# Prompt attention rewritten as one pipeline over heads and groups

## The chip, the cores and the metric

One core of a Trainium2 chip runs one program. The metric is the device time of one execution in microseconds (us), lower is better. TensorE (PE) multiplies matrices from the on-chip memory SBUF into the accumulators PSUM (eight banks), VectorE (DVE), ScalarE (ACT) and GpSimd (POOL) work on elements, and SyncE (SP) issues DMA transfers. All wait for each other by semaphores only.

## The reference, cut to what matters

The program is one inference step of a decoder layer for a prompt of 512 tokens and 32 sampled tokens. All arithmetic is float32. The part that matters here is attention over the prompt:

```
proj = rmsnorm(x) @ w_in           # queries, keys, values, gates of two mixers
# (B) differential attention, 8 heads, two maps each
a = softmax(q1 k1' * s + bias) - lam * softmax(q2 k2' * s + bias)   # causal, 512 x 512
o_b = rmsnorm(a @ v, subln_g) * (1 - lam_init)
# (A) sparse attention, 16 heads in 4 groups that share keys; three branches each
o_c = softmax(q kc' * s + bias) @ vc     # 32 compressed rows
o_s = softmax(q ks' * s + bias) @ vs     # selected blocks: at 512 tokens all of them, causal
o_w = softmax(q kw' * s + bias) @ vw     # the last 512 tokens, causal
o_a = g0 * o_c + g1 * o_s + g2 * o_w     # sigmoid gates per token and head
o = sigmoid(ga) * o_a + sigmoid(gb) * o_b
y = x + o @ w_o, then a squared-ReLU MLP
```

## The kernel before, in words

The program runs five stages with a barrier between them: `project` (the combined projection), `compress` (compressed keys and values), `prompt_attention`, `decode_attention` (the sampled tokens against the cache) and `finish` (output projection and MLP). Within a stage each engine has its own list of instructions, unrolled by Python loops; the order of the lists and the semaphores are the whole schedule.

`prompt_attention` (L1048) works in units. A unit is one query tile of 128 tokens for two score maps at once (two 64-row halves of the PE array): the two maps of one differential head (`Head`, L1137, 8 heads x 4 tiles = 32 units), or two heads of a group for one of the three branches (`group_units`, L1117; per group 2 pairs of heads x 4 tiles x 3 branches = 24 units, 4 groups = 96 units). With the tile number t the number of keys grows from 128 to 512; the compressed branch has 32 keys. I call the 12 units of one pair of heads half a group.

A unit goes through five steps. TensorE multiplies scores into two of the four banks of `ps_s`. VectorE adds the bias, negates, and takes the minimum (`tensor_tensor_reduce`, L1469 and L1510) into the SBUF slot `sc`. ScalarE takes the exponential in place with its row sum (L1383, L1405). TensorE turns the probabilities by transposing them into the two banks of `ps_t` (L1281, L1327), ScalarE and VectorE copy them out to `p_t` (L1418, L1392, L1477), and TensorE multiplies them by the values into `ps_o` (L1291, L1338). Then VectorE scales and sums: for a head one instruction (L1535); for a tile of a group, after its third branch, three tiny ones for the coefficients (L1483 to L1486) and two for the sum into `oa` (L1496, L1499). For a head VectorE also mixes the two maps before they are turned (`head_mix`, L1519), so only one half is turned.

The stage has two loops with different depths. The heads' loop (L1355 on TensorE, L1421 on ScalarE, L1564 on VectorE) turns a unit four units after its scores and turns the next head's queries and keys in between, from a written list `TURN_ORDER` (L1154) that deals the two `ps_t` banks out one after the other. The groups' loop (`run`: L1342, L1394, L1548) turns a unit two units after its scores. In it bank 0 of `ps_t` belongs to the first half of a unit and to ScalarE's copy, bank 1 to the second and VectorE's. At the start of every group (`turn_group`, L1294, called at j = 0 and 24 of each pair of groups) TensorE turns the queries and keys of the group into the banks of the scores (`ps_s`), after the last unit of the group before, and waits until ScalarE and VectorE have copied them (L1310, L1311).

Around the units: SyncE loads `lv` and `gain` first (L1166 to L1168), TensorE and VectorE wait for these five loads (L1245, L1455), then SyncE loads groups 0 and 1, the later heads, the constants of the next stage, and groups 2 and 3 as slots come free (L1206 to L1214). The first four heads are loaded by `compress`. GpSimd (L1219) squares and sums the heads' output `ob` once all heads are done and multiplies in `gain`; ScalarE takes the square root in group 1 (L1440), VectorE the reciprocal (L1592); GpSimd then scales and gates `ob` per group (L1238, L1240). VectorE merges a whole group in two instructions of 128 x 1024 elements, `oa * ga` and `+ ob` (`merge_group`, L1537), at j = 10 of the next group's loop and once after the last. SyncE then stores `oa` to DRAM, from which `finish` reads.

Of the kernel before, what the change touches and what calls it, by code (L numbers as in the profile page):

```python
# [98 lines left out]
class Shared:  # L99

    def __init__(self, nc, ctx):
# [8 lines left out]
        self.h_in = [s.sem(f"h_in{u}") for u in range(HEADS_AT_ONCE)]  # L111
        self.consts_in, self.q_in, self.kc_in = s.sem("consts_in"), s.sem("q_in"), s.sem("kc_in")
# [4 lines left out]
    def weights(self, ctx):  # L117

        s, nc = self.space, self.space.nc
        self.first = s.ctx_sb(ctx, "first", [P, 2 * KT * CW])  # L120
        self.hi = s.ctx_sb(ctx, "hi", [P, 2, KT * CW], F32R)
        self.lo = s.ctx_sb(ctx, "lo", [P, 2, KT * CW], F32R)
        self.pe_t = s.ctx_sb(ctx, "pe_t", [P, 2, 2 * KT])
        self.w2 = s.ctx_sb(ctx, "w2", [P, 2, 2, DK])
        self.k_gain = s.ctx_sb(ctx, "k_gain", [P, DK])

class Ahead:

    def __init__(self, s, ctx):
# [11 lines left out]
        self.gain = s.ctx_sb(ctx, "gain", [P, DV])  # L143
# [488 lines left out]
def compress(nc, d, shared):  # L632
# [3 lines left out]
    with ExitStack() as ctx:  # L636
# [48 lines left out]
        def _(sp):  # L685
# [14 lines left out]

            sp.wait_ge(w1_lo, 2)
# [346 lines left out]
def prompt_attention(nc, d, shared):  # L1048

    with ExitStack() as ctx:
# [12 lines left out]
        ks_t = s.sb("ks_t", [P, SEQ])  # L1064
        kw_t = s.sb("kw_t", [P, SEQ])
        kc_t = s.sb("kc_t", [P, CHP])
# [10 lines left out]
        osq = s.sb("osq", [P, DHEADS, DV])  # L1077
        ssum = s.sb("ssum", [P, QT * DHEADS])
        merge = s.sb("merge", [P, 2, QT, HPG * DK])
        ident = shared.ident  # L1080
        lam, gain = shared.ahead.lam, shared.ahead.gain
        lv = s.sb("lv", [P, 4, DD])
# [4 lines left out]
        consts_in, begun, begun_keys = s.sem("consts_in"), s.sem("begun"), s.sem("begun_keys")  # L1087
        g_in = [s.sem(f"g_in{u}") for u in range(2)]
        h_in = shared.h_in
        keys_mm, q_copied, k_copied = s.sem("keys_mm"), s.sem("q_copied"), s.sem("k_copied")  # L1090
        scores_mm, scored, probs, turned, values_mm = (
            s.sem(n) for n in ("scores_mm", "scored", "probs", "turned", "values_mm"))
        p_copied = [s.sem(f"p_copied{k}") for k in range(2)]
        mixed, h_turned, h_values = s.sem("mixed"), s.sem("h_turned"), s.sem("h_values")
        h_copied = {"act": s.sem("h_copied_act"), "dve": s.sem("h_copied_dve")}
# [3 lines left out]
        o_sq, o_root, ob_scale, ob_gated = s.sem("o_sq"), s.sem("o_root"), s.sem("ob_scale"), s.sem("ob_gated")  # L1099
        merge_in, merge_step, merged = s.sem("merge_in"), s.sem("merge_step"), s.sem("merged")  # L1100
# [3 lines left out]
        HP = HPG // 2  # L1104
        DU, DM = QT, QT
        NU, NM = HP * QT * 3, HP * QT
        N_BASE, M_BASE = DHEADS * DU, DHEADS * DM
        G_LOADS, H_LOADS = 12, 4

        class Unit:  # L1110
            def __init__(self, lhs, rhs, bias, width, values, out, clamp, m, br, nbr):
                self.lhs, self.rhs, self.bias, self.width, self.values, self.out = lhs, rhs, bias, width, values, out
                self.clamp, self.m, self.br, self.nbr = clamp, m, br, nbr

        HALF = [slice(DK * x, DK * (x + 1)) for x in range(2)]

        def group_units(u, m0):  # L1117
            out = []
            for hp in range(HP):
                for t in range(QT):  # L1120
                    m = m0 + QT * hp + t
                    lhs = [q_t[x, hp, P * t:P * (t + 1)] for x in HALF]
                    n = P * (t + 1)
                    first = P * (QT - 1 - t)
                    c0 = first + CMP_BLOCK - 1
                    two = [strip[:, u, 2 * hp + x, :] for x in range(2)]
                    cb = [x[:, c0:c0 + CMP_STRIDE * (CHP - 1) + 1:CMP_STRIDE] for x in two]
                    sb = [x[:, first:SEQ] for x in two]
# [1566 lines left out]
```

## Time and profile before

| what | us |
|---|---|
| median of 3 runs (lowest, highest) | 1886.89 (1885.14, 1887.85) |
| the profiled execution | 1906.63 |
| its span | 1904.9 |
| heads' scores of prompt attention | 699.4 to 771.2 |
| groups' part of prompt attention | 783.1 to 1067.4 |

| engine | busy us in the span | share |
|---|---|---|
| TensorE | 1760.4 | 92% |
| VectorE | 821.1 | 43% |
| ScalarE | 589.1 | 31% |
| GpSimd | 76.9 | 4% |

PEld is TensorE's weight load, which overlaps the matmuls. In a timeline row a bracket says how long the engine had been idle before the row and what released it. The granted clock over the whole span is 0.923.

### The profile page before, as it was taken

The numbers are of one execution on the slowest core, as the hardware profiler recorded it, in microseconds if no ns is written. First come the engines' busy times: TensorE is split into PE (matmuls) and PEld (weight loads), VectorE is DVE, ScalarE is ACT, GpSimd is POOL, SyncE is SP. The second block draws the span as 40 slices with busy tenths as digits, with TensorE's granted clock in tenths as the row PEclk, the third lists the DMA queues.
The fourth block names the chain that finished last, engine by engine and source line by source line (L and its number), as shares of the span: only waits on it lengthen the run. The fifth ranks groups of instructions, "written<-read, shape, count | busy, mean of one in ns | idle before, by whom it ended". The sixth has DMA issues, their size and how long they took to land. (4 is left out here: it accounts for less than half of the span.)

```text
span 1904.9 us, 32764 instructions
## 1 busy us (share of the span) xinstructions
PE 1760.4 (92%) x13036; PEld 1486.1 (78%) x13036; DVE 821.1 (43%) x1874; ACT 589.1 (31%) x1228; POOL 76.9 (4%) x88
## 2 busy tenths in 40 slices
PE   7999999987999968899899899999958899999998
PEld 4888888876888855677787677777658899999998
DVE  4576532113333338747645544344333542234322
ACT  4232212212333236545544223233222332123210
POOL 0000000000000000512000000000010000000000
PEclk9999999978999979967867799999969899999999
DMA  9755444304331344503301199988361233433331
GB/s 284 265 185 157 158 157 146 130 30 100 96 81 26 94 136 136 182 1 102 102 1 34 54 356 343 324 286 331 150 202 45 89 110 110 132 108 103 98 88 47
DMA packets 187833, 265.68 MB, mean 139 GB/s; under 512 B 35245, under 2 KB 117485, under 8 KB 187590
## 3 DMA queue, kind: packets, MB, share of 16 engines
q1 hardware_dynamic: 183598, 244.36, 39.9%
q10 hardware_dynamic: 3096, 11.21, 1.6%
q0 software_dynamic: 1024, 8.59, 1.4%
q8 instruction: 71, 1.16, 0.3%
q14 instruction: 44, 0.36, 0.1%
HBM read 241.04 MB, written 42.60 MB: 149 GB/s over the span
## 5 line engine op out<-in xcount | busy, mean ns | idle before, releaser
L586 PE MATMUL pj_ps<-all_hi,pj_xh 128*128 128x512 f32 x480 | 191.0, 398 | 1.6 <-DVE all_lo L482 1.6
L588 PE MATMUL pj_ps<-all_hi,pj_xl 128*128 128x512 f32 x480 | 189.4, 395 | 0.0
L587 PE MATMUL pj_ps<-all_lo,pj_xh 128*128 128x512 f32 x480 | 189.4, 395 | 0.0
L2590 PE MATMUL fi_ps<-fi_fh,fi_wh 128*128 128x272 f32 x512 | 150.5, 294 | 7.0 <-DVE fi_fl L2518 7.0
L2590 PE MATMUL fi_ps<-fi_th,fi_wh 128*128 128x272 f32 x512 | 149.2, 291 | 1.0 <-DVE fi_tl L2448 1.0
L2592 PE MATMUL fi_ps<-fi_fh,fi_wl 128*128 128x272 f32 x512 | 150.0, 293 | 0.0
L2591 PE MATMUL fi_ps<-fi_fl,fi_wh 128*128 128x272 f32 x512 | 149.4, 292 | 0.0
L2592 PE MATMUL fi_ps<-fi_th,fi_wl 128*128 128x272 f32 x512 | 148.8, 291 | 0.0
L2591 PE MATMUL fi_ps<-fi_tl,fi_wh 128*128 128x272 f32 x512 | 148.1, 289 | 0.0
L1383 ACT ACTIVATE pa_sc<-pa_sc,pa_nmax 128x32 f32<-128x32 f32 (+4 forms) x192 | 90.7, 473 | 131.4 <-DVE pa_nmax L1469 130.6
L2070 ACT ACTIVATE de_slot<-de_ps_t 128x512 f32<-128x512 f32 (+5 forms) x124 | 62.9, 514 | 216.7 <-PE de_ps_t L1910 105.6
L2178 DVE COPY de_slot<-de_ps_t 128x512 f32<-128x512 f32 (+4 forms) x112 | 69.2, 623 | 129.6 <-PE de_ps_t L1910 73.2
L586 PEld LDWEIGHTS pj_ps<-all_hi,pj_xh 128*128 128x128 f32 x480 | 90.3, 188 | 25.4 <-issue 2.8
L965 PE MATMUL cm_ph<-cm_xh,all_hi 128*128 128x512 f32 x256 | 108.4, 423 | 0.2 <-DVE cm_xl L829 0.2
L588 PEld LDWEIGHTS pj_ps<-all_hi,pj_xl 128*128 128x128 f32 x480 | 90.3, 188 | 21.4
L587 PEld LDWEIGHTS pj_ps<-all_lo,pj_xh 128*128 128x128 f32 x480 | 90.3, 188 | 20.7
L2590 PEld LDWEIGHTS fi_ps<-fi_fh,fi_wh 128*128 128x128 f32 x512 | 98.4, 192 | 7.4 <-issue 7.4
L2386 ACT ACTIVATE fi_wh<-all_big 128x2048 fp32r<-128x2048 f32 x30 | 57.2, 1908 | 150.3 <-PE fi_ps L2592 150.3
L966 PE MATMUL cm_ph<-cm_xl,all_hi 128*128 128x512 f32 x256 | 101.5, 396 | 0.0
L967 PE MATMUL cm_ph<-cm_xh,all_lo 128*128 128x512 f32 x256 | 101.3, 396 | 0.0
L2591 PEld LDWEIGHTS fi_ps<-fi_fl,fi_wh 128*128 128x128 f32 x512 | 98.5, 192 | 0.0
L2592 PEld LDWEIGHTS fi_ps<-fi_fh,fi_wl 128*128 128x128 f32 x512 | 98.3, 192 | 0.0
(332 smaller groups left out, 3528.4 us busy)
## 6 DMA issues: line engine op xcount, KB each, us to landing
de_dv<-in_cache_diff SPq DMA_DIRECT2D x64, 512.0 KB, 10.0
all_big<-in_w_in SPq DMA_DIRECT2D x14, 2048.0 KB, 8.8
all_big<-in_cache_nsa SPq DMA_DIRECT2D x96, 256.0 KB, 5.6
de_dk<-in_cache_diff SPq DMA_DIRECT2D x48, 512.0 KB, 9.4
all_big<-in_w_up SPq DMA_DIRECT2D x16, 1024.0 KB, 5.4
all_big<-in_w_down SPq DMA_DIRECT2D x16, 1024.0 KB, 5.5
all_first<-in_cache_nsa SPq DMA_DIRECT2D x32, 256.0 KB
all_win<-in_cache_win SPq DMA_DIRECT2D x32, 256.0 KB, 10.8
```

The costliest lines, as they stand in the source:

```text
L586: pe.matmul(ps[:, t, 0:width], xh[:, k, xk], hi(k), start=k == 0, stop=False)
L587: pe.matmul(ps[:, t, 0:width], xh[:, k, xk], lo(k), start=False, stop=False)
L588: ins = pe.matmul(ps[:, t, 0:width], xl[:, k, xk], hi(k), start=False, stop=k == KT - 1)
L965: pe.matmul(o, w1h[k][:, kt, col], mh, start=first, stop=False)
L966: pe.matmul(o, w1h[k][:, kt, col], ml, start=False, stop=False)
L967: ins = pe.matmul(o, w1l[k][:, kt, col], mh, start=False, stop=last)
L1383: nc.scalar.activation(sc[:, j % 4, a, 0:x.width], sc[:, j % 4, a, 0:x.width], ACT.Exp, scale=-1.0, bias=nmax[:, j % 4, a:a + 1], accum_ou ...
L2070: ins = nc.scalar.activation(slot[rows, g % 4, cols], ps_t[rows, g % 4, cols], ACT.Copy)
L2178: ins = nc.vector.tensor_copy(slot[rows, g % 4, cols], ps_t[rows, g % 4, cols])
L2590: pe.matmul(o, hi[:, k, :], a_hi[:, k, tok], start=k == 0, stop=False)
L2591: pe.matmul(o, hi[:, k, :], a_lo[:, k, tok], start=False, stop=False)
L2592: ins = pe.matmul(o, lo[:, k, :], a_hi[:, k, tok], start=False, stop=k == kts - 1)
```

## The change

The two loops of `prompt_attention` become one list `UNITS` of 128 units, which all engines walk in steps of two with one depth (`LAG = 4`) and six `sc` slots. What it does, part by part:

- Scores run four units ahead of turning in the groups too. All uses of the two `ps_t` banks, heads' and groups', come from one `TURN_ORDER`; a use waits for the copy of the use two before it (`place`).
- The next head's and next group's queries and keys are turned inside the loop into `ps_t` (`FILL`): for a group four and two units before its first unit, its second pair's queries two units after. `keys` has four slots and `kc_t` two.
- VectorE's `merge_group` is gone. GpSimd merges each tile of 128 x 128 after VectorE has combined it, in two instructions; `oa` is stored in two halves per group. The first `merge` load waits for the heads' squares (`o_sq`), whose scratch `osq` now lies in `merge`.
- `lv` and `gain` are loaded in `compress`, ahead of its page loads; TensorE no longer waits for them.

```diff
@@ compress, SyncE
+            for j, name in enumerate(("lambda_q1", "lambda_k1", "lambda_q2", "lambda_k2")):
+                sp.dma_start(shared.lv[:, j, :], spread(d[name], P)).then_inc(shared.lv_in, 16)
+            sp.dma_start(shared.gain[:], spread(d["diff_subln"], P)).then_inc(shared.lv_in, 16)
             sp.wait_ge(w1_lo, 2)
@@ prompt_attention
+        UNITS = [Head(n) if n < NH else Branch(n) for n in range(N)]
+        LAG = 4
+        FILL = {}
+        for h in range(1, DHEADS):
+            FILL[QT * h - 2] = [("q", h, 0), ("k", h, 0)]
+        for g in range(GROUPS):
+            b, x = first_of(g), DHEADS + g
+            FILL[b - 4] = [("q", x, 0), ("k", x, 0)]
+            FILL[b - 2] = [("k", x, 1), ("c", x, 0)]
+            FILL[b + 2] = [("q", x, 1)]
+        TURN_ORDER = [("q", 0, 0), ("k", 0, 0)]
+        for j in range(0, N + LAG, 2):
+            TURN_ORDER += FILL.get(j, [])
+            for n in (j - LAG, j - LAG + 1):
+                if 0 <= n < N:
+                    TURN_ORDER += UNITS[n].turns
+        VALUES_AFTER = {n: [n - 2 if n < NH else n - 1] for n in range(2, N + 1)}
@@ SyncE
+            sp.wait_ge(o_sq, 1)
+            load_merge(0)
             for g in range(GROUPS):
                 if g + 2 < GROUPS:
+                    sp.wait_ge(combined, NH + 2 * QT * (g + 1))
                     load_group(g + 2, g % 2)
+                for hp in range(2):
+                    sp.wait_ge(merged, 2 * QT * g + QT * (hp + 1))
+                    at = HPG * DK * g + P * hp
+                    sp.dma_start(tok(d["oa"][0:SEQ, at:at + P]), oa[:, g % 2, :, P * hp:P * (hp + 1)]).then_inc(oa_out[g % 2], 16)
@@ GpSimd
+                for hp in range(2):
+                    for t in range(QT):
+                        mine = oa[:, g % 2, t, P * hp:P * (hp + 1)]
+                        pool.wait_ge(combined, NH + 2 * QT * g + QT * hp + t + 1)
+                        step(nc.gpsimd.tensor_tensor(mine, mine, merge[:, 0, t, P * hp:P * (hp + 1)], ALU.mult))
+                        nc.gpsimd.tensor_tensor(mine, mine, ob[:, t, 2 * g + hp, :], ALU.add).then_inc(merged, 1)
@@ TensorE
-            pe.wait_ge(consts_in, 80)
+            for j in range(0, N + LAG + 2, 2):
                 for n in (j, j + 1):
+                    if n < N:
+                        scores(UNITS[n])
+                for x in FILL.get(j, []):
+                    fill(x)
+                for n in (j - LAG, j - LAG + 1):
+                    if 0 <= n < N:
+                        turn(UNITS[n])
+                    for v in VALUES_AFTER.get(n, []):
+                        values(UNITS[v])
@@ ScalarE
+            for j in range(0, N + LAG, 2):
+                exps(j); copy queries of FILL[j]; copy(j - LAG); exps(j + 1); copy(j - LAG + 1)
+                if j == NH + NG + 2:      # square root of ssum, as before in group 1
@@ VectorE (from NH on)
+                score(j); copy keys of FILL[j]; copy(j - LAG); score(j + 1); copy(j - LAG + 1)
+                scale_branches for j - LAG, j - LAG + 1 where a tile closes
+                combine_branches for j - LAG - 2, j - LAG - 1 where a tile closes
-            merge_group(GROUPS - 1)
```

The last two parts are written short: each call stands under its bounds (`if j < N` and the like), and the heads' units have `mix_maps` and `combine_head` where they had them before. VectorE's combine of a group's tile is unchanged but for its wait (`valued` of its own unit).

## Rows read from the trace of the kernel before

**Rows 1.** The page's slices: granted clock of TensorE in 40 equal slices, in tenths

```profile
PEclk9999999978999979967867799999969899999999
```

**Rows 2.** Windows of prompt attention: each engine's busy us, clock, DMA share, GB/s

```profile
699.40:771.20 71.80, 57.37 (x374) 38.24 (x375) 59.66 (x242) 48.31 (x156) 0.00 (x0) 0.95 0.63 175
771.20:783.10 11.90, 9.28 (x78) 8.20 (x76) 8.13 (x25) 5.70 (x14) 2.66 (x2) 1.00 0.14 45
783.10:1067.40 284.30, 264.06 (x1583) 212.30 (x1579) 170.02 (x654) 132.54 (x489) 45.76 (x47) 0.74 0.20 64
992.30:1020.70 28.40, 24.28 (x194) 19.99 (x192) 21.05 (x82) 15.44 (x60) 0.00 (x0) 0.99 0.15 47
948.50:992.30 43.80, 43.02 (x213) 34.80 (x211) 20.49 (x84) 17.32 (x62) 4.21 (x2) 0.57 0.02 8
```

**Rows 3.** Windows of the six stretches at the slow clock in the groups' pass

```profile
784.40:791.20 6.80, 5.89 (x26) 4.10 (x25) 2.84 (x18) 3.76 (x19) 6.08 (x9) 0.50 0.98 343
808.30:845.90 37.60, 37.12 (x159) 29.43 (x159) 17.82 (x74) 14.36 (x55) 5.99 (x9) 0.50 0.01 2
862.90:883.40 20.50, 19.23 (x76) 13.60 (x75) 14.74 (x43) 7.62 (x30) 6.11 (x3) 0.50 0.55 158
924.40:931.20 6.80, 5.81 (x26) 4.17 (x24) 2.74 (x17) 3.76 (x18) 0.00 (x0) 0.50 1.07 338
948.30:985.80 37.50, 37.48 (x162) 29.61 (x161) 16.58 (x71) 13.74 (x53) 4.21 (x2) 0.50 0.03 11
1019.90:1057.50 37.60, 37.57 (x163) 29.71 (x163) 16.59 (x71) 13.62 (x53) 2.35 (x1) 0.50 0.05 17
```

**Rows 4.** Timeline (start, us, instruction, count): TensorE's rates at full clock

```profile
1063.61 1.86 PEld L1338 LDWEIGHTS pa_ps_o<-pa_vs,pa_p_t 128*128 128x128 f32 x16
...
1061.17 0.86 PEld L1327 LDWEIGHTS pa_ps_t<-all_ident,pa_sc 128*128 128x128 f32 x8 [0.37 <-ACT pa_sc L1383]
...
1012.97 1.02 PE L1317 MATMUL pa_ps_s<-pa_kw_t,pa_q_t 64*128 64x512 f32 x4
...
1000.65 0.60 PE L1317 MATMUL pa_ps_s<-pa_kw_t,pa_q_t 64*128 64x256 f32 x4
...
1003.63 0.41 PE L1317 MATMUL pa_ps_s<-pa_kc_t,pa_q_t 64*128 64x32 f32 x4
```

**Rows 5.** Timeline: SyncE around the stage's start, TensorE's first turning

```profile
397.46 16.33 SPq L383 DMA_DIRECT2D scratch_g<-pj_y  x5
...
434.29 30.07 SPq L203 DMA_DIRECT2D all_big<-in_cache_nsa  x16
...
689.85 0.36 SPq L1167 DMA_DIRECT2D pa_lv<-in_lambda_q  x1
...
696.59 1.94 PE L1261 MATMUL pa_ps_t<-all_ident,all_big 128*128 128x128 f32 x8 [9.69 <-DMA all_gain<-in_diff_subln]
```

**Rows 6.** Timeline of single instructions ahead of three slow stretches

```profile
806.41 1.89 POOL L1224 TENSOR_TENSOR pa_osq<-pa_ob 128x1024 f32<-128x1024 f32 x1
...
806.51 1.81 DVE L1483 TENSOR_SCALAR pa_coef<-pa_rsum 128x6 f32<-128x6 f32 x1
...
858.24 1.28 ACT L1383 ACT_TABLE_LOAD   x1
...
1013.10 1.21 DVE L1542 TENSOR_TENSOR pa_oa<-pa_oa,pa_merge 128x1024 f32<-128x1024 f32 x1
...
1014.35 1.22 DVE L1546 TENSOR_TENSOR pa_oa<-pa_oa,pa_ob 128x1024 f32<-128x1024 f32 x1
```

**Rows 7.** Groups of GpSimd's instructions, and the one line L1483: min/median/max ns

```profile
L1240 POOL TENSOR_TENSOR pa_ob<-pa_ob,pa_merge 128x1024 f32<-128x1024 f32 x4 | 9.4, 2354 | 145.8 <-DMA pa_merge<-scratch_gb 145.7
...
L1228 POOL TENSOR_TENSOR pa_osq<-pa_osq 128x128 f32<-128x128 f32 x4 | 1.8, 452 | 0.3
...
L1483 DVE TENSOR_SCALAR pa_coef<-pa_rsum x32: 147/149/1894, 791.7 to 1064.7; 128x6 f32<-128x6 f32 x32
```

**Rows 8.** Timeline: TensorE's last values of the stage

```profile
1065.45 1.95 PE L1338 MATMUL pa_ps_o<-pa_vw,pa_p_t 128*128 128x64 f32 x16
```

More of the change, by code:

```diff
@@ L1270, in head_scores, with scores @@
+            def scores(x):
+                for need in x.needs:
+                    pe.wait_ge(copied[copier[TURN[need]]], copies[TURN[need]])
+                    stand()
                 if x.n >= 2:
-                    pe.wait_ge(scored, 4 + 2 * (x.n - 1))
+                    pe.wait_ge(scored, 2 * (x.n - 1))
                 for a in range(2):
@@ L1313, in scores, with turn @@
-            def scores(x, j, n):
-                pe.wait_ge(scored, 2 * n + 2)
-                for a in range(2):
-                    ins = pe.matmul(ps_s[:, 2 * (j % 2) + a, 0:x.width], x.lhs[a], x.rhs[a], start=True, stop=True)
-                ins.then_inc(scores_mm, 1)
-            def turn(x, j, n):
-                for a in range(2):
-                    pe.wait_ge(probs, 2 * n + a + 1)
-                    pe.wait_ge(p_copied[a], n - N_BASE + 1)
+            def turn(x):
+                for a, entry in enumerate(x.turns):
+                    if x.n < NH:
+                        pe.wait_ge(mixed, x.n + 1)
+                    else:
+                        pe.wait_ge(probs, 2 * x.n + a + 1)
+                    stand()
+                    bank = place(entry)
@@ L1325, in turn, with values @@
                     for k, v in enumerate(x.values):
                         r = v.shape[0]
-                        ins = pe.transpose(ps_t[0:r, a, P * k:P * (k + 1)], sc[:, j % 4, a, P * k:P * k + r], ident[:])
+                        ins = pe.transpose(bank[0:r, P * k:P * (k + 1)], sc[:, x.n % 6, a, P * k:P * k + r], ident[:])
                     ins.then_inc(turned, 1)
-            def values(x, j, n, m0):
-                if x.br == 0:
-                    pe.wait_ge(combined, m0 + x.m + 1)
-                for a in range(2):
-                    pe.wait_ge(p_copied[a], n - N_BASE + 2)
+            def values(x):
+                if x.opens_tile and x.tile >= 2:
+                    pe.wait_ge(combined, x.tile - 1)
+                    stand()
+                for a, entry in enumerate(x.turns):
+                    pe.wait_ge(copied[copier[TURN[entry]]], copies[TURN[entry]])
@@ L1366, in _ @@
[L1366 to L1373 removed]
+                        ins = pe.matmul(x.out[a], x.p_t[a][0:r, P * k:P * (k + 1)], v, start=k == 0, stop=k == len(x.values) - 1)
+                ins.then_inc(valued, 1)
```

534 lines of the change are left out of this document (213 added, 321 removed).

## The prediction

> **What bounds the kernel now.** I read the page's slices first: TensorE is busy in nearly every slice, but its clock row [rows 1] has its longest run of low digits (6 to 9) between slices 17 and 24. That is prompt attention, the stage that the change rewrites. The windows by stage come next [rows 2]. The heads' pass (699.4 to 771.2 us) runs at 0.95 of full clock; VectorE is the fullest engine there (59.66 of 71.80). The groups' pass (783.1 to 1067.4, 284.3 us) is 15% of the span, has TensorE busy 264 of it and VectorE 170, and its clock averages 0.74. So TensorE bounds this pass, and half of the time it does so at 1.2 GHz. The reader is to see this in two halves of a group (a half: 12 units, two heads of the group, four query tiles): the one at 992.3 takes 28.4 us at clock 0.99, the same work at 948.5 takes 43.8 us at 0.57. The slow clock lies in six stretches [rows 3]: 6.8 + 37.6 + 20.5 + 6.8 + 37.5 + 37.6 = 146.8 us.
>
> The timeline before each of them tells what starved TensorE [rows 6]. Before 1019.9 VectorE does the two merges of a whole group (L1542, L1546; 2.5 us in a row) while scores of the widest tile wait; the same pair stands ahead of 948.3. 784.4 and 924.4 follow a change to the next group, where the pipeline is emptied. Before 862.9 ScalarE loads two tables around the square root. Before 808.3 a VectorE instruction of 6 elements (L1483) takes 1.81 us, its usual time being 0.149 (the median in [rows 7]), and it ends when GpSimd's L1224 does.
>
> **The change part by part.** The sum is against the profiled execution, 1906.6 us (span 1904.9); the median of the runs is 1886.9, 19.7 less. Where that difference lies the profile can't say, so I take the saving over in us.
>
> 1. *Stage start.* TensorE's first transposes wait 9.69 us, in the end for `diff_subln`, whose load SyncE issues behind four others from 689.85 [rows 5]. With the five loads moved into compress and the wait dropped, TensorE can start at about 690.2 instead of 696.6: its heads' data were issued long before. VectorE's lambda steps move along. Saved 6.3. Price of the moved issues: five of about 0.45 us on SyncE, which sits idle from 413.8 to 434.3 there [rows 5]; hidden.
>
> 2. *Heads to groups.* The heads' loop keeps its order and its lag of four. Now the last head scores start at 771 and the first group scores reach VectorE at 783.1, 11.9 us later, and only 8.2 us of weight loads lie between [rows 2]. Of these 2.3 are group 0's turning and first scores, so 5.9 are heads' work that remains. Saved 11.9 - 5.9 = 6.0. The clock, high here, has no gap to fall in.
>
> 3. *Half a group at the full clock.* TensorE's own rates [rows 4]: a value matmul 1.86/16 = 0.116 us (its weight load sets it), a transpose 0.86/8 = 0.107, scores of 512 keys 1.02 us per unit, of 256 0.60, of 32 0.41. A half has 96 value matmuls (11.1), 48 transposes (5.2) and eight wide and four narrow score pairs; by these rows, less the modelled end of each, about 6.4. Sum 22.7, and 17 turning transposes per group add 0.9 per half: floor 23.6. The other bound is the 28.4 of today [rows 2], which holds one 2.5 us merge on VectorE; without it 25.9. VectorE's work is 170/8 = 21.3 per half, under 20.1 once its four merges (4 x 2.43) are GpSimd's. I take 25.5: near today's row without the merge, since a lag of four instead of two removes TensorE's short waits for copies and exponentials but not the handshake over the two `ps_t` banks. Bounds 23.6 to 28.4. The added waits: a turn waits for the copy out of its bank two turns ago, and behind it stand the values of the unit before; VectorE's `copy` stands behind `score`, and behind a combine at each third unit (up to 2 us), which the light tiles can't cover. That is why I don't take the floor.
>  Eight halves: 8 x 25.5 = 204. The tail after the last scores, with five units in flight instead of three, grows by about 1.5. Against 284.3: 78.8 saved, if the clock stays high.
>
> 4. *Merges on GpSimd.* Sixty-four more instructions of 128 x 128; the nearest row takes 0.45 us (L1228) [rows 7]. Per group 16 x 0.45 = 7.2 beside 4.3 for the scaling and gating of `ob` (the gating row takes 2.35); a group lasts over 50, so they are hidden. Group 0's merges wait for the square root in group 1, and SyncE waits behind them; its next duty (the loads for group 3) is due only some 20 units later. At the stage's end VectorE's two merges (2.5) become two GpSimd instructions (0.9): saved about 1.5 after the last values [rows 8]. Lower bound 0, upper 2.5.
>
> 5. *What GpSimd does to VectorE.* L1483 took up to 1.894 us where 0.149 is usual [rows 7], next to a GpSimd instruction [rows 6]. The new GpSimd instructions last 0.45, and 64 of VectorE's small ones (L1483, L1486) are exposed: from 0 to 64 x 0.45 = 29 us on VectorE, which has 204 - 160 = 44 to spare. I take 2 on the path.
>  The Trainium skill (SBUF — State Buffer, Who interferes with whom) states the rule behind such a row: VectorE and GpSimd share one pair of ports as an exclusive lock, and a VectorE instruction with two SBUF inputs, or in a two-port mode, waits for a whole GpSimd instruction. It speaks against moving merges to GpSimd: by the rule alone each hit costs what is left of the other's instruction. The trace agrees for L1483 and shows none of it for the scores, which read one operand from PSUM. It would make the sum 27 us less good only if each of the 64 were hit in full and on the path.
>
> 6. *The clock.* Every us at 1.2 GHz costs: the 948.5 half has 37.5 us of it and takes 43.8 instead of 25.5, so 18.3/37.5 = 0.49 us per us. The change removes the causes ahead of four stretches (two merges, two changes of group: 88.7 us). The square root's table loads and the long GpSimd instructions at the pass's start remain, with four units of slack. I take 25 us of slow clock: 12 lost. Bounds 0 and 146.8 us: 0 to 72.
>  The Trainium skill (TensorE: Matmul & The Clock Gate, Part 1) says that the gate throttles by default and sustained activity releases it. By this alone the pass should be quick once gaps are gone. The trace agrees only in part: at 1.2 GHz the pass has TensorE busy 37.48 of 37.50 us [rows 3] and stays slow.
>
> Sum: 6.3 + 6.0 + 78.8 + 1.5 - 2 - 12 = 78.6. Forecast 1887 - 79 = 1808 us.
>
> **The rivals.**
> A. *The clock falls as often as now.* For it: slow stretches of 37 us last from one half's start to its widest tile whatever started them, and a steady mixture of light and heavy units may offer new low moments. Against it: the heads' pass, at lag four and with TensorE far less full, stays at 0.95. Saving 92.6 - 72 = 21: 1866.
> B. *Ports and banks.* GpSimd's locks land on the path (27 more), or the two banks hold a half at 28.4 (23 more). For it the 1.81 us row; against it the spare time of VectorE. 1835.
> C. *No slow clock and nearly the floor* (24 per half): 92.6 + 12 - 2 = 103 saved: 1784.
> D. *Slower: once down, the clock stays down.* Today it comes back at the widest tile, where two score pairs of 512 stand together (the stretches end at 845.9, 883.4, 985.8, 1057.5). If turns and values of older, lighter units interleaved there keep it low, the halves run like the one at 948.5: 8 x 43.8 = 350 instead of 204, 54 slower than before: 1941. It decides from the sixth such half on (18.3 x 5.06 = 92.6). Against it: the order on TensorE keeps both score pairs side by side.
> E. *Not what it says*: a group's keys turned early need its loads. Group 2's are issued once group 0 is combined, 20 units ahead of use, over 40 us, and today's issues take 11. Not likely; a wait of 5 us twice would cost 10.
>
> **How the numbers follow.** The likeliest case 0.62; A 0.16; B 0.12; C 0.05; D 0.05 (E inside the likeliest). The likeliest one's own range: 1790 to 1828. The 80% range reaches most of C and B and stops short of A's middle: 1784 to 1854. A measurement of this kernel tells about 0.2% (3.8 us) from no change; all but D lie beyond it on the fast side: faster 0.93, same 0.02, slower 0.05.
>
> **What would show it.** Step 1: first transposes of the stage at 690 and no wait for `diff_subln`. Step 2: no stretch without scores between heads and groups. Step 3: first scores of successive halves 24 to 27 us apart where the clock is 1. Step 4: no VectorE instruction of 128 x 1024, GpSimd 0.45 us per merge. Step 5: the maximum of the small `coef` instructions and whether TensorE waits follow. Step 6: granted clock of the pass above 0.9 and low stretches of 20 to 40 us in all. I am wrong if the clock stays near 0.74 (then A), if halves at full clock take 28 or more (B), or if stages outside prompt attention change by over 5 us, which nothing here touches.

## The result, and the profile after

The changed kernel takes 1856.95 us (median of 4, 1854.2 to 1862.6) against 1887.37 for the kernel before beside it: ratio 0.984 [0.980, 0.988]. A second pair gave 1865.8 (10 executions, 1856.5 to 1876.9) against 1895.4 (19, 1870.3 to 1906.4): 0.989 [0.984, 0.994]. So 30 us were gained where 79 were forecast, and the time lies above the range (1784 to 1854). Ratios leave out executions over 1.5% above the fastest of their kernel, so they can differ from the quotient of the medians.

The profiled execution of the changed kernel has a span of 1853.0 us. Its granted clock by slices, which answers [rows 1]:

```profile
PEclk9999999988899989969999899999878899999999
```

The low digits of slices 17 to 24 are nearly gone; one 6 is left. The windows that answer [rows 2] (busy us of TensorE, its weight loads, VectorE, ScalarE, GpSimd; granted clock; DMA share; GB/s), in this order: the heads, the groups' pass, the last half of a group (no fills), an odd half (the second of its group; the fills for the next group are in it), the half with the long slow stretch, and that stretch:

```profile
691.80:772.70 80.90, 60.22 (x401) 41.20 (x401) 64.13 (x255) 51.83 (x164) 0.00 (x0) 0.96 0.55 150
772.70:1023.70 251.00, 226.80 (x1631) 184.09 (x1629) 167.19 (x660) 133.01 (x494) 76.38 (x110) 0.90 0.26 80
988.60:1012.50 23.90, 21.92 (x176) 17.95 (x174) 17.11 (x78) 13.86 (x56) 3.66 (x8) 1.00 0.04 12
931.70:959.70 28.00, 25.54 (x206) 20.84 (x205) 20.52 (x84) 16.18 (x61) 6.89 (x11) 1.00 0.15 48
800.90:841.80 40.90, 38.65 (x211) 32.31 (x210) 20.50 (x84) 17.01 (x61) 15.69 (x20) 0.66 0.21 73
797.80:828.50 30.70, 30.70 (x145) 26.74 (x144) 12.19 (x55) 10.79 (x42) 18.54 (x23) 0.50 0.38 136
```

The pass fell from 284.3 to 251.0 us and its clock rose from 0.74 to 0.90. But a half at full clock takes 28.0 us, hardly less than the 28.4 of [rows 2], which held a merge of 2.5. The stage's start answers [rows 5]:

```profile
688.68 1.94 PE L1317 MATMUL pa_ps_t<-all_ident,all_big 128*128 128x128 f32 x8 [3.13 <-PEq L96]
```

TensorE starts 7.9 us earlier, 1.3 of it because the stage ahead ended earlier, and waits for no load. The merges and the small steps on the coefficients answer [rows 7] (first two rows: busy us, mean ns; the others: min/median/max ns, first and last start):

```profile
L1281 POOL TENSOR_TENSOR pa_oa<-pa_oa,pa_merge 128x128 f32<-128x128 f32 x32 | 14.6, 457 | 95.9 <-DVE pa_oa L1476 95.6
L1282 POOL TENSOR_TENSOR pa_oa<-pa_oa,pa_ob 128x128 f32<-128x128 f32 x32 | 14.6, 456 | 2.5
...
L1464 DVE TENSOR_SCALAR pa_coef<-pa_rsum x32: 148/160/1978, 786.2 to 1020.9; 128x6 f32<-128x6 f32 x32
L1465 DVE RECIPROCAL pa_coef<-pa_coef x32: 190/191/195, 786.7 to 1021.0; 128x6 f32<-128x6 f32 x32
L1466 DVE TENSOR_TENSOR pa_coef<-pa_coef,pa_gates x32: 165/166/2161, 786.9 to 1021.3; 128x6 f32<-128x6 f32 x32
```

What the stretched steps do, ahead of the stretch that answers [rows 6] (timeline; brackets are idle time and releaser):

```profile
790.94 1.10 DVE L1464 TENSOR_SCALAR pa_coef<-pa_rsum 128x6 f32<-128x6 f32 x1
...
792.09 1.89 POOL L1260 TENSOR_TENSOR pa_merge<-pa_ob 128x1024 f32<-128x1024 f32 x1
792.30 1.71 DVE L1466 TENSOR_TENSOR pa_coef<-pa_coef,pa_gates 128x6 f32<-128x6 f32 x1
...
795.14 0.69 DVE L1426 CUSTOM_DVE_ANT_0 pa_sc<-pa_ps_s,pa_strip 128x512 f32<-128x512 f32 x1
...
795.87 0.72 ACT L1377 ACTIVATE pa_sc<-pa_sc,pa_nmax 128x512 f32<-128x512 f32 x1 [5.11 <-DVE pa_nmax L1426]
```

Two steps of 6 elements hold VectorE for 2.8 us where 0.33 is usual; the next score starts at 795.14, and ScalarE has had nothing for 5.11 us.

The second thing to see is the fills (L1317): two sets of transposes fill both `ps_t` banks.

```profile
948.35 0.60 PE L1317 MATMUL pa_ps_t<-all_ident,pa_ks 128*128 128x128 f32 x4
948.41 0.61 ACT L1377 ACTIVATE pa_sc<-pa_sc,pa_nmax 128x384 f32<-128x384 f32 x1 [0.61 <-DVE pa_nmax L1426]
...
949.03 0.60 ACT L1377 ACTIVATE pa_sc<-pa_sc,pa_nmax 128x384 f32<-128x384 f32 x1
...
949.63 0.58 ACT L1383 ACTIVATE pa_q_t<-pa_ps_t 128x512 f32<-128x512 f32 x1
950.25 0.42 PEld L1340 LDWEIGHTS pa_ps_t<-all_ident,pa_sc 128*128 128x128 f32 x4 [1.54 <-ACT pa_q_t L1383]
```

The turned queries were in PSUM by 948.5, but ScalarE did two exponentials first, and TensorE stood 1.54 us.

### The profile page after: what moved, and what is told of

It is laid out like the page before. It is cut to its first block and busy times, and to the rows that moved or that the text cites. A ratio compares the mean times of both kernels' runs of the same rounds, so it can differ in the third digit from the quotient of the medians.

```text
span 1853.0 us, 32827 instructions
## 1 busy us (share of the span) xinstructions
PE 1713.2 (92%) x13036; PEld 1449.2 (78%) x13036; DVE 812.3 (44%) x1866; ACT 587.5 (32%) x1228; POOL 105.8 (6%) x152
## 5 line engine op out<-in xcount | busy, mean ns | idle before, releaser
L1377 ACT ACTIVATE pa_sc<-pa_sc,pa_nmax 128x32 f32<-128x32 f32 (+4 forms) x256 | 126.0, 493 | 125.7 <-DVE pa_nmax L1426 125.3
L1340 PE MATMUL pa_ps_t<-all_ident,pa_sc 128*128 128x128 f32 (+1 forms) x464 | 81.7, 297 | 39.2 <-ACT pa_p_t L1391 14.4
L1340 PEld LDWEIGHTS pa_ps_t<-all_ident,pa_sc 128*128 128x128 f32 (+1 forms) x464 | 51.9, 144 | 65.5 <-ACT pa_p_t L1391 19.2
```

What stands on the lines that cost most here:

```text
L1340: ins = pe.transpose(bank[0:r, P * k:P * (k + 1)], sc[:, x.n % 6, a, P * k:P * k + r], ident[:])
L1377: nc.scalar.activation(tile, tile, ACT.Exp, scale=-1.0, bias=nmax[:, x.n % 6, a:a + 1], accum_out=x.sums[a]).then_inc(probs, 1)
```

## The clock account

Every execution comes with its span and mean granted clock. The us at 1.2 GHz in it are 2 x (1 - clock) x span, and each costs 0.49 us by the prediction's row (a line through 71 executions of the kernel before, from 1869.6 us at 0.944 to 1908.8 at 0.924, gives 0.44). Span less 0.49 times these is what I call the time at full clock. It is a reckoned time; no execution ran so. Its standard deviation is 1.4 to 4.3 us for every kernel, and the kernel before has 1762.2 to 1763.0 in each of its five sets, so runs on different chips can be compared in it:

| kernel | n | median us | clock | at full clock |
|---|---|---|---|---|
| before, five sets on four chips | 71 | 1893.4 | 0.931 | 1762.6 |
| changed, second pair | 10 | 1865.8 | 0.944 | 1763.6 |
| e1 early loads alone | 10 | 1888.2 | 0.933 | 1760.4 |
| e2 merges alone | 10 | 1867.8 | 0.944 | 1762.1 |
| e5 changed, merges back | 10 | 1894.4 | 0.933 | 1766.8 |
| e4 changed, GpSimd idle | 4 | 1841.5 | 0.954 | 1760.9 |
| e3 changed, copies first | 4 | 1842.6 | 0.950 | 1750.3 |
| e6 e3, fills spread | 4 | 1849.4 | 0.949 | 1754.8 |
| e12 changed, no fills | 4 | 1849.9 | 0.947 | 1752.9 |
| e9 changed, coefficients late in PSUM | 4 | 1850.8 | 0.955 | 1768.8 |
| e7 e3 and that | 4 | 1821.0 | 0.960 | 1748.0 |
| e13 e7 again | 4 | 1819.2 | 0.961 | 1748.3 |
| e11 e3, coefficients late in SBUF | 4 | 1824.3 | 0.960 | 1751.9 |
| e10 e7, VectorE's copies first too | 10 | 1877.1 | 0.934 | 1755.0 |
| e8 before, with merges and coefficients of e7 | 10 | 1888.9 | 0.935 | 1765.2 |

At full clock the changed kernel is as long as the one before. Its 30 us are 54 us less at 1.2 GHz. With 0.44 as the price the two still lie within 2 us of each other; of what the kernels with the highest clock (e7, e13) gain on the kernel before, some 6 us more then count as full clock and as much less as clock.

## The experiments

**The parts one by one.** The stage's start alone:

```
-            for j, name in enumerate(("lambda_q1", ...)):          # in prompt attention
-            pe.wait_ge(consts_in, 80)
+            for j, name in enumerate(("lambda_q1", ...)):          # in compress, into shared.lv, gain
```

> The kernel before with one part of the change alone: the five small loads of the lambda vectors and the gain are issued in the stage ahead, into places of their own, and TensorE does not wait for them. Theory (step 1 of the prediction): the stage's first transposes start 6.3 us earlier and everything behind them moves with them, so 6 to 7 us less than before, ratio 0.9966. Rival: the start is earlier, but the stage's clock falls at other places, and the whole moves by 15 us or more in either direction, which would make every difference of this size in this kernel a matter of where the clock falls.

1888.2 us, ratio 0.9996 [0.995, 1.005]. In the trace the first transposes start at 687.76 instead of 696.59, and the groups' first score 5.5 us earlier. The time can't tell 6 us from none; at full clock it is 2 us better, which is not clear of its scatter. The edit does what it says, and its worth is below what the clock's wandering lets one see.

The merges alone, on the kernel before:

```
-                    if j in (10, NU + 10) and 2 * i + j // NU:
-                        merge_group(2 * i + j // NU - 1)           # VectorE
+                        step(nc.gpsimd.tensor_tensor(mine, mine, merge[...], ALU.mult))   # by tile
+                        nc.gpsimd.tensor_tensor(mine, mine, ob[...], ALU.add).then_inc(merged, 1)
```

> The kernel before with the merges of a group (gate times result, plus the head's part) moved from VectorE to GpSimd, tile by tile, and nothing else. Theory (steps 4 and 6): the moved work is hidden, the end of the stage comes 1.5 us earlier, and the slow-clock stretches that began behind VectorE's two merge instructions (1.2 us each) no longer begin: with one of the stretches of 37.5 us gone that is 1.5 + 18 = 20 us less than before, ratio 0.990. Rival 1: the clock falls elsewhere as often, only 1.5 us less, ratio 0.999. Rival 2: GpSimd's work beside VectorE's small instructions costs more than it saves, since GpSimd now works through the whole group: VectorE's two small coefficient instructions are hit 10 times and not 4 or 5, and the kernel is 2 to 10 us slower.

1867.8 us, ratio 0.990 [0.986, 0.995]: 23 us less, all in the clock. The theory gave 20. The same edit undone in the changed kernel:

> The changed kernel with the merges back on VectorE as the kernel before has them: two 128x1024 instructions of 1.2 us for each group, in the middle of the next one and at the end. Moving them to GpSimd alone took 23 us off the kernel before, with the granted clock of the whole up from 0.934 to 0.944. Theory: they do the same here, two more long slow-clock stretches, clock 0.942 or lower, 15 to 25 us slower than the changed kernel, so 1872 to 1882. Rival: with scores four units ahead TensorE has work in hand over a stall of 2.4 us on VectorE, the clock stays, and it is 1.5 us slower at the end alone.

1894.4 us, ratio to before 1.003 [0.998, 1.008]; to the changed kernel 28.6 us slower, more than expected. The merges by themselves carry the change's whole gain. The traces show where: in those of before and e1 four pairs of merges stand at full clock (at 941.1 and 1013.1; 924.9 and 996.9), and each is followed by a stretch of 37.5 us at 1.2 GHz (from 948.3, 1019.9; 932.0, 1003.6). In e2's trace the longest stretch of the pass is 23.9 us, and the pass has 44 us at 1.2 GHz for the 147 of before. In e5's trace the pairs stand inside short slow stretches, and one of the three is followed by a longer one (17.1 us from 932.1). For e5, the pass of its profiled execution, whose time is the lowest of ten (1875.4):

```profile
773.60:1037.10 263.50, 238.03 (x1631) 192.83 (x1629) 175.22 (x666) 133.14 (x495) 48.43 (x48) 0.86 0.24 76
```

The changed kernel once more, to see whether its work is shorter at equal clock:

> The changed kernel once more, beside the kernel before on one chip, to have the pair as often as the experiments. So far the spans and granted clocks of the runs (19 of before, mean clock 0.934, and 4 of after, 0.950) say: take 0.49 us off for each us that the clock stood at 1.2 GHz, and before comes to 1763 us, after to 1766. Theory: the changed kernel's whole gain is the clock, the work at full clock takes the same time, so this difference stays within 5 us again while the medians differ by 25 to 35 us. Rival: that was chance in four runs, and at equal clock the changed kernel is 10 us or more faster.

Medians 29.6 us apart, 1763.6 against 1762.2 at full clock: it is not.

**Why a half takes 28 us.** ScalarE's order in the groups' part:

```
-                exps(UNITS[j]); <query fills>; copy(UNITS[j - LAG])
-                exps(UNITS[j + 1]); copy(UNITS[j - LAG + 1])
+                <query fills>; copy(UNITS[j - LAG]); exps(UNITS[j])
+                copy(UNITS[j - LAG + 1]); exps(UNITS[j + 1])
```

> The changed kernel, in the groups' part only ScalarE's order changed: the copy of unit j-4's turned probabilities stands ahead of the exponentials of unit j, and the copy of j-3 ahead of those of j+1, where in the changed kernel it stands behind. Theory (copies queued behind exponentials hold both PSUM banks of the turned probabilities): a half of a group takes 26 us at full clock instead of 28, 8 halves save 12 to 16 us against the changed kernel, so 1841 to 1845. Rival 1: what costs is that the transposes of the next group's queries and keys take turns in the same two banks, whatever ScalarE's order: within 3 us of the changed kernel. Rival 2: the exponentials now wait behind a copy that waits for TensorE, the pipeline is one unit shorter, and it is slower than the changed kernel by 5 us or more.

1842.6 us, ratio 0.980 [0.972, 0.989], 13 less at full clock. From the first score to the last of the groups' part, TensorE's listed waits for copies fall from 22.8 to 11.5 us (19.0 in the kernel before). The same odd half takes 26.7 and the same place of the timeline has TensorE stand 0.49 instead of 1.54:

```profile
918.40:945.10 26.70, 25.70 (x207) 21.08 (x206) 20.42 (x85) 15.92 (x62) 6.86 (x11) 1.00 0.19 59
```

```profile
934.39 0.60 PE L1317 MATMUL pa_ps_t<-all_ident,pa_ks 128*128 128x128 f32 x4
934.59 0.60 ACT L1383 ACTIVATE pa_q_t<-pa_ps_t 128x512 f32<-128x512 f32 x1 [0.52 <-PE pa_ps_t L1317]
...
935.24 0.20 PEld L1340 LDWEIGHTS pa_ps_t<-all_ident,pa_sc 128*128 128x128 f32 x2 [0.49 <-ACT pa_q_t L1383]
```

Spreading the fills over four steps instead of two:

```
-            FILL[b - 4] = [("q", x, 0), ("k", x, 0)]
-            FILL[b - 2] = [("k", x, 1), ("c", x, 0)]
+                for k, one in enumerate((("q", x, 0), ("k", x, 0), ("k", x, 1), ("c", x, 0))):
+                    FILL[b - 8 + 2 * k] = [one]                    # groups 1 to 3
```

> The kernel with ScalarE's copies first (1842.6 us), and the next group's queries and keys turned one set to a step, 8, 6, 4 and 2 units ahead of the group, where the changed kernel turns two sets in each of the last two steps. Theory (two sets in one step fill both PSUM banks, so that the next probabilities wait for their copies: 1.38 us at fill to turn in a half, against 0.13 between plain turns): a group of 24 units is 2 us shorter, the three groups but the first save 5 to 8 us, 1835 to 1838. Rival: every single set stalls as long as a pair did, since its copy stands behind a score or an exponential all the same: no change, or 3 us slower by the extra switches.

1849.4 us, ratio 0.980 [0.967, 0.993]: a miss, 4.5 us worse at full clock. An odd half took 28.3 instead of 26.7, and TensorE's waits for copies rose from 11.5 to 17.0 us: single fills stall as pairs do, and there are more steps with one. What they cost in all was measured by leaving them out:

```
-        for g in range(GROUPS):                                     # FILL
+        for g in range(1):
```

> The changed kernel in which the queries and keys of the second to fourth group are not turned nor copied at all: their scores are computed from the first group's, so the stored results are wrong; everything else stays. Theory (the forecast's half of a group at 25.5 us counted 0.9 us for this work, and it costs more, since it takes turns in the two PSUM banks of the probabilities: 28.0 us for a half with it, 23.9 for the last one without): the odd halves fall to 24 us, the even ones to 26.5, three groups save 5.5 us each, 16 us, the clock rises a little: 1842 to 1850. Rival (the work is hidden as forecast, and what costs is only that ScalarE's copies of probabilities stand behind exponentials): the halves stay at 27 us or more, and it saves 3 x 1.8 = 5 us: 1858 to 1862.

1849.9 us, ratio 0.981 [0.970, 0.991], as the theory had it; at full clock 10.7 less for three groups, 3.6 a group or 1.8 a half, twice the forecast's 0.9. An odd half without them (not the 24 us expected):

```profile
870.40:897.00 26.60, 23.95 (x194) 19.62 (x193) 20.00 (x81) 15.33 (x60) 6.88 (x11) 1.00 0.03 9
```

So the 28.0 us can be read as the 24.6 that the forecast gave to a half without fills, some 1.8 for the fills and 1.5 for copies behind exponentials (1.3 in that half, 1.7 by the time at full clock). The last two are measured, each with the other cost still there; no run left out both, and the 24.6 remain the forecast's.

**What holds the slow clock.** GpSimd's arithmetic left out (only its waits stay, so the results are not normalised or merged):

> The changed kernel without GpSimd's arithmetic in prompt attention: the squares of the heads' results, the scaling, the gating and the merges are left out, so the stored results are not normalised or merged; all waits, loads and stores stay. Theory (GpSimd's work slows VectorE's small instructions, 10 of 32 hit at up to 2 us each, and one such stall starts the long slow-clock stretch of 30.7 us in the second half of the first group): the mean of the two small instructions falls from 0.69 to 0.16 us, that stretch is gone (15 us), a half at full clock takes 27 us instead of 28 (8 us): 1830 to 1842. Rival: VectorE has room for these stalls and the clock falls anyway; within 3 us of the changed kernel's time.

1841.5 us, ratio 0.983 [0.973, 0.992]. The small step is never stretched, and the half that took 40.9 takes 29.6; halves at full clock stay at 27.6 to 28.0, against the expected 27:

```profile
L1450 DVE TENSOR_SCALAR pa_coef<-pa_rsum x32: 148/154/161, 788.6 to 1004.2; 128x6 f32<-128x6 f32 x32
...
799.40:829.00 29.60, 27.15 (x205) 21.36 (x204) 20.39 (x85) 16.18 (x61) 0.00 (x0) 0.94 0.41 149
```

GpSimd beside VectorE costs some 24 us, by the clock (one of the four executions took 1863.6, so the size is rough). The cure that keeps its work, on top of e3:

```
-                for n in (j - LAG, j - LAG + 1): ... scale_branches(UNITS[n])
-                step(nc.vector.tensor_scalar(out..., rsum..., TINY, None, ALU.max))
+                scale_branches(x)                                   # in combine_branches, behind its wait
+                raw = ps_o[:, x.tile % 2, 6 * DK:6 * DK + 6]
+                step(nc.vector.tensor_scalar(raw..., rsum..., TINY, None, ALU.max))
```

> The kernel with ScalarE's copies first (1842.6 us), and VectorE's two small coefficient steps taken off SBUF alone: the maximum and the reciprocal are kept in PSUM, in unused columns of the tile's bank once TensorE has left it. Theory (instructions that read and write SBUF alone are the ones that GpSimd's work stretches; with an operand in PSUM none of 192 scores was): the three small steps stay at 0.13 to 0.2 us each, the slow stretch of 19 us in the second half of the first group goes as it did with GpSimd idle (3.4 us there), 6 to 10 us less, 1833 to 1837. Rival: the last of them still writes SBUF and is stretched as often, or the clock falls in that half all the same; within 3 us of 1842.6.

1821.0 us (1820.1 to 1822.3), ratio 0.966 [0.954, 0.977], better than expected. No slow clock is left in the groups' part, and halves take 25.1 and 26.7 (groups' pass, an even and an odd half, the step now in PSUM):

```profile
773.40:983.00 209.60, 204.86 (x1631) 167.12 (x1629) 155.99 (x657) 131.63 (x494) 76.38 (x110) 1.00 0.30 96
874.20:899.30 25.10, 24.85 (x201) 20.35 (x200) 18.66 (x82) 16.02 (x62) 4.60 (x7) 1.00 0.41 124
899.30:926.00 26.70, 25.74 (x206) 20.75 (x204) 20.29 (x85) 16.09 (x61) 6.84 (x11) 1.00 0.25 76
...
L1467 DVE TENSOR_SCALAR pa_ps_o<-pa_rsum x32: 144/156/168, 789.1 to 983.0; 128x6 f32<-128x6 f32 x32
```

The reciprocal and the product, which now read PSUM, are not stretched either (203 to 204 and 164 to 167 ns). But two things had changed, the place of the step and its memory. The later place alone (`raw = coef[...]`):

> The kernel that ran in 1821.0 us differs from the one with ScalarE's copies first (1842.6) in two things: the coefficients' maximum and reciprocal are kept in PSUM, and the three small steps stand later, right ahead of the tile's combination. Here they stand later but stay in SBUF. Theory (SBUF to SBUF steps are what GpSimd stretches): the maximum and the product are stretched as before, means of 0.3 us instead of 0.16, and the time stays at 1838 to 1846. Rival (the place was what mattered: two units later the small steps no longer stand between a score and the next): 1820 to 1826 with the small steps stretched all the same.

1824.3 us, ratio 0.962 [0.956, 0.967]: the rival. The step is still stretched, to 1787 ns, and nearly all of the gain is there:

```profile
L1467 DVE TENSOR_SCALAR pa_coef<-pa_rsum x32: 147/161/1787, 788.0 to 989.5; 128x6 f32<-128x6 f32 x32
```

My reason for e7 was thus wrong in its size: PSUM cures the stretching wholly, but was worth some 3 us, which is hardly clear of the scatter; the place, behind the next step's copies and scores instead of ahead of them, was worth 18, all in the clock. Why the place keeps the clock up so well stays open. Summed over both stretched steps the stretching is 6.8 us in this trace and 10.5 in e3's, and the worst case is as bad as before: two stretched steps again stand between a copy and the next score.

```profile
806.47 0.29 DVE L1444 COPY pa_p_t<-pa_ps_t 128x128 f32<-128x128 f32 x1 [0.61 <-PE pa_ps_t L1340]
806.68 1.79 DVE L1467 TENSOR_SCALAR pa_coef<-pa_rsum 128x6 f32<-128x6 f32 x1
...
808.73 1.70 DVE L1469 TENSOR_TENSOR pa_coef<-pa_coef,pa_gates 128x6 f32<-128x6 f32 x1
...
811.56 0.19 DVE L1429 CUSTOM_DVE_ANT_0 pa_sc<-pa_ps_s,pa_strip 128x32 f32<-128x32 f32 x1
```

Yet only 6.8 us at 1.2 GHz follow here (from 809.9), where 30.7 followed in the changed kernel and 20.5 in e3.

The late coefficients in PSUM on the changed kernel, with ScalarE's order as it was:

> The changed kernel with the coefficients' maximum and reciprocal in PSUM and nothing else (ScalarE's order as the change has it). Theory 1 (two separate causes): it loses the 30.7 us stretch of slow clock as with GpSimd idle, halves stay at 28 us since the copies still stand behind the exponentials: 1838 to 1846, as with GpSimd idle (1841.5). Theory 2 (the copies' order matters only after a stretched small step): halves fall to 25 to 26 us without the new order and it comes to 1825 or less.

1850.8 us, ratio 0.976 [0.971, 0.981]: theory 1, somewhat slower than it said. Fewer slow stretches (25 us in the pass for 49), halves at 28 to 29 us: the two cures are separate, and together they give at least what they give one by one (45 us; 23 and 15).

The same coefficients on the kernel before, with the merges on GpSimd:

> The kernel before, without the pipeline of the change, with two edits: the merges on GpSimd by tile, as the change has them (alone 1867.8 us), and the coefficients' maximum and reciprocal kept in PSUM (which took the kernel with the pipeline and ScalarE's copies first from 1842.6 to 1821.0). Theory (the pipeline itself is worth nothing at full clock, what is worth something is a VectorE whose small steps GpSimd does not stretch): full-clock time 1762 less 5 for the stretches, clock 0.955 to 0.960 as there, so 1833 to 1845 us. Rival: without scores four units ahead the drains at the groups' borders (16.8 us for a tile of 10) start the slow clock anyway: clock 0.944 to 0.950, 1855 to 1868, and then the pipeline is what lets the cure work.

1888.9 us, ratio 0.996 [0.992, 0.999]: the rival, and worse than it said; 21 us slower than e2, with the clock at 0.935. No small step is stretched in its trace (156 to 168 ns), and still the pass has 92 us at 1.2 GHz where e2's has 44: stretched steps are not all that starts slow clock. TensorE's waits for copies did not grow (19.8 us, 21.7 in e2), so why late coefficients cost the clock at a lag of two stays open. e2 and the changed kernel (1867.8, 1865.8) say that the pipeline with the earlier start is worth nothing by itself; e8 and e9 (1888.9, 1850.8) say that it is what lets the coefficients' new place work.

The fastest kernel with VectorE's copies of keys and probabilities ahead of its scores:

> The fastest kernel so far (ScalarE's copies first, coefficients in PSUM, 1821.0 us), with VectorE's order changed too: the copies of the turned keys and of the probabilities stand ahead of the score instructions of the same step. Theory (the stalls left at the turned keys, 0.72 and 0.38 us each behind a score of 0.7 us, go): a half with fills takes 24.3 us instead of 25.0 to 26.7, 6 to 10 us less, 1811 to 1815. Rival: VectorE now waits for TensorE's transposes with a finished score in PSUM behind it, the scores two units on come late, and it is 5 us or more slower.

1877.1 us, ratio 0.992 [0.988, 0.996]: the rival, far harder than its 5 us. Seven us at full clock, and the clock does the rest; one even half:

```profile
825.80:869.00 43.20, 42.26 (x195) 34.23 (x195) 19.18 (x82) 19.97 (x64) 14.52 (x20) 0.54 0.38 112
```

What helped on ScalarE harms on VectorE: its waits for TensorE's transposes rise from 26.4 to 97.9 us in the groups' part, with finished scores in PSUM, and TensorE, which in e7's list never waits for VectorE to read scores, now does so for 6.6 us.

The fastest kernel on another chip:

> The fastest kernel (ScalarE's copies first, the coefficients' steps later and in PSUM) once more on another chip. Theory: 1819 to 1824 us as before (1820.1 to 1822.3), granted clock 0.960. Rival: the four runs were a lucky place of the slow-clock stretches, and it spreads as the changed kernel does (1854 to 1877), with a median of 1830 or more.

1819.2 us (1817.2 to 1821.2), ratio 0.964 [0.955, 0.973]. The fastest kernel beats the changed one by 45 us, and its eight executions on two chips differ by 5 us where the ten of the changed kernel differ by 20: with the groups' part free of slow stretches there is less left to wander.

## Why the prediction was wrong

Step 3 failed, the forecast of 25.5 us for half a group at full clock: the halves took 27.0 by the same reckoning and were no shorter than those before. The rest of the miss is a base with bad luck, a tail left out of the sum, and more slow clock than forecast. Between the two profiled executions 51.9 us of span were saved, 26.7 less than forecast; between the medians 30.

1. *Base.* I took the saving over in us from an execution 19.7 above the median and said that the profile couldn't place the difference. It can: its clock is 0.923 where the kernel's mean is 0.931, 30 us more at 1.2 GHz, 15 us of time; and the first profile after (0.952) was one of the good ones of its kernel. Of the 78.8 us of step 3 some 72 were slow clock (146.8 x 0.49), so the base's bad luck was counted as gain: some 21 us of the miss lie between the profiled pair and the medians.
2. *Step 1, stage start*: 6.3 forecast, 6.6 in the trace. Right.
3. *Step 2, heads to groups*: 6.0 forecast, 2.8 found (80.9 us from first head score to first group score, 83.7 before). Turning waits there for the copies of the fills: in the window 691.8 to 772.7, by the list of TensorE's waits (us in total, times, longest; the same waits for queries and keys came to 10.6 us before):

```profile
PE pa_ps_t L1340 <- DVE pa_keys L1434: 10.8, 8, 3.0
PE pa_ps_t L1340 <- ACT pa_q_t L1383: 4.4, 7, 0.7
```

4. *Step 3, half a group at full clock*: the step that failed, by the handshake over the two `ps_t` banks that it mis-sized. Eight halves at 25.5 were forecast, 204 us. They took 239.8 with 48.9 at the slow clock, so 215.8 at full clock, 27.0 each; the two with no slow clock at all took 28.0 and 29.1 (from 931.7 and 873.4). The same reckoning over the kernel before gives 276.9 - 0.49 x 146.8 = 205.0, 25.6 each: taken over all eight halves and not from the one at 992.3 [rows 2], the rows said that there was next to nothing to gain. Nor are the two halves of [rows 2] quite the same work: the one at 948.5 has 213 matmuls and the turning for the next group in it, the one at 992.3 has 194 and a merge. The 0.49 has the forecast's own 25.5 in it. With the measured 28.4 in its place the same two rows give (43.8 - 28.4)/37.5 = 0.41, and by that price a half took 27.1 before and 27.5 after: nothing gained either. The lag did remove the waits for probabilities that it was meant to (4.5 us of weight loads behind `sc` in the half at 992.3, none listed in the half at 931.7); the fills in the banks of the probabilities (twice their price, e12) and copies behind exponentials (e3) put more back, 11 us in all by the price of 0.49, which ate the gains of steps 1, 2 and 4. Rival B named the banks, at 23 us.
 And a slip: 8 x 25.5 covers first score to last, while the 284.3 us also hold the tail behind the last scores, 7.4 us (1060.0 to 1067.4). I added 1.5 and forgot the 7.4; the tail measured 11.2. That is 9.7 of the miss. VectorE's under 20.1 us per half was low too: only three of the four merges stood in the pass (the fourth starts at 1068.9), and 167.2 us were measured, 20.9 per half.
5. *Step 4, merges*: hidden, 0.457 us each, the stage's end 2.4 us shorter (5.8 us from last values to decode's first matmul, 8.2 before): right as a term. But this is the part that carries the gain, which the text put into step 6 and spread over four causes. e2 and e5 say 23 and 29 us for it alone, the handovers' share is none that can be seen. That 37.5 us of slow clock follow a stall of 2.5 us on VectorE is seen in before and e1; why the stretch is so long is not.
6. *Step 5, stretched small steps*: 2 us on the path was the forecast, 24 us what GpSimd's work costs (e4), nearly all by the clock. The Trainium skill (SBUF — State Buffer, Who interferes with whom) states the rule that speaks against moving merges to GpSimd: the engine that comes second to the shared ports waits for the whole instruction of the other. The rows agree: none of 32 is hit with GpSimd idle or with one operand in PSUM, and a hit lasts until GpSimd's instruction ends (875.20 + 2.35 and 875.61 + 1.98 below). The merges are still better there, since their pieces are short: the 2.35 us gating costs a step 1.8 us, a merge of 0.46 costs the next step 0.1:

```profile
875.20 2.35 POOL L1276 TENSOR_TENSOR pa_ob<-pa_ob,pa_merge 128x1024 f32<-128x1024 f32 x1 [4.62 <-DMA pa_merge<-scratch_gb]
875.61 1.98 DVE L1464 TENSOR_SCALAR pa_coef<-pa_rsum 128x6 f32<-128x6 f32 x1
877.64 0.46 POOL L1281 TENSOR_TENSOR pa_oa<-pa_oa,pa_merge 128x128 f32<-128x128 f32 x1
877.84 0.27 DVE L1466 TENSOR_TENSOR pa_coef<-pa_coef,pa_gates 128x6 f32<-128x6 f32 x1
```
7. *Step 6, clock*: 25 us at 1.2 GHz forecast in the pass, 48.9 found, 30.7 of them behind the two stretched steps at 790.9 and 792.3. That the pass would stay above 0.9 held barely (0.90). The amount was off by 12 us. The price was on the high side: lines through the executions of one kernel give 0.44 for the kernel before and 0.34 to 0.59 for the six kernels with ten executions.
8. *Stages outside*: the prediction named a change of over 5 us there as a sign of being wrong. It was 7.1 us: 1.3 ahead of the stage and 5.8 behind decode's first matmul (829.3 before, 823.5 after). Behind it the traces have 87.2 and 78.1 us at 1.2 GHz, so 4.5 of the 5.8 are the clock; the traces of the other kernels have 75 to 89 there, though the edits leave the work of those stages as it is.

Together: 3.2 (step 2) + 11.8 (halves) + 9.7 (tail) + 12.0 (48.9 us at the slow clock at 0.49, for the 12 forecast) = 36.7, less the 2 of step 5, which lie in the halves, less 8.3 that came unforecast (5.8 behind the stage, 1.3 before it, 1.2 in steps 1 and 4): 26.4 of the 26.7 us. How halves and clock share their 23.8 us hangs on the price.

The mechanism drawn wasn't false: with ScalarE's order and the coefficients' place mended the pass takes 209.6 us at clock 1.00, where the forecast had 205.5 before the clock (212.9 with the forgotten tail). What I hadn't looked for was what each engine would have to finish first at the new lag.

## What to carry to other kernels

Reckon each execution down to full clock before comparing: a gain that is only in the clock, and one that the clock hides, both show at once, in spans and clocks that every run lists. Take the price of slow clock from measured rows alone, and try the result with the price of a line too. Price a repeated stretch from all its repetitions, not from the cleanest. When a pipeline is lengthened, reorder the in-order engines by what the next engine waits for (copies out of a shared PSUM bank first on ScalarE) and put small bookkeeping steps late; then test each order, since the same move on VectorE cost 56 us, and the late steps cost 21 us at a lag of two.

## What the runs showed of the hardware

Of three steps of 6 elements side by side, GpSimd's work stretches the maximum (to 1978 ns) and the product (2161), never the reciprocal (190 to 195), though all three read and write SBUF alone. With the result in PSUM the maximum stays at 144 to 168 ns, and the product, with one input there, at 164 to 167. The mean granted clock of one kernel wanders from 0.920 to 0.947 over 71 executions and the time by 39 us, 2%; eight executions of the fastest kernel stay within 5 us.
